# Expert weights in runs of 16 KB: four successive rows to a partition, and the turned rows of x and of the activations taken with a step of four columns

## The chip, the cores and the metric

The kernel runs on one core of one Trainium2 chip, in float32 throughout. The metric is the device time of one execution in microseconds (us), the median of three runs.

## The reference

One layer of a diffusion backbone with 128 context tokens and 512 latent tokens of 1024 features: adaLN modulation, two groups of attention heads, an output projection, and then an expert-choice mixture of 16 experts. The last part is the one that matters here:

```python
def expert_choice_moe(h, w_router, w_gate, w_up, w_down):
    B, T, D = h.shape
    cap = CAPACITY_FACTOR * T // N_EXPERTS
    logits = jnp.einsum('btd,de->bte', h, w_router, preferred_element_type=jnp.float32)
    aff = jax.nn.softmax(logits, axis=-1)
    g, idx = lax.top_k(jnp.swapaxes(aff, 1, 2), cap)
    xg = jax.vmap(lambda hb, ib: hb[ib])(h, idx)
    a = jnp.einsum('becd,edf->becf', xg, w_gate)
    u = jnp.einsum('becd,edf->becf', xg, w_up)
    y = jnp.einsum('becf,efd->becd', jax.nn.silu(a) * u, w_down) * g[..., None].astype(h.dtype)
    return jax.vmap(lambda yb, ib: jnp.zeros((T, D), yb.dtype).at[ib.reshape(-1)].add(yb.reshape(-1, D)))(y, idx)
```

`h = rms_norm(x, g_pre_ffn) * (1 + scale) + shift`, with shift and scale from the modulation. Each expert has three weights of 1024 x 1024 (4 MB each), takes 64 latent rows and 16 context rows, and is computed for both kinds of token.

## The kernel before

**Stages.** The weights of the modulation (`w_ada`), of the input projection and of the output projection come in units of 2 MB through a ring of six slots of 16 KB per partition. SyncE issues all these loads in the order of `UNITS`; between two of them, in `load_consts`, it issues ten small loads (sinks, router weights `wr`, gains). The projection loop runs over 15 products (`project`, L632 and L656), with the rest of the modulation (`ada`, L582) put between them. Attention follows, then the output projection (L810), the router, and the experts from about 394 us on.

**Experts.** An expert has six halves of 2 MB: gate, up and down, halves 0 and 1. `expert_weight` (L476) loads one: partition p takes rows 128c + p for four successive c, so a partition has four runs of 4 KB that lie 512 KB apart in memory. Up and down have two slots each in the ring, the gate weights four (two more slots in `reg2_qt`, named `reg_qt` in the profile). SyncE waits until TensorE has used a slot and then issues its next load (`refill`), in the order up(e+1), gate(e+3), down(e+1). Its waits are all that holds these loads back.

**TensorE's order.** `product_c` (L968) multiplies the context rows with one half, in 16 steps of 128 x 256 weights to four quarters of the output partitions; `product_l` (L954) does the latent rows in 16 steps of 128 x 512. The weights are the moving operand, 32 rows of x or of activations the stationary one. Each float32 product is two matmul instructions in the trace. `expert(e)` runs up(e), half 0 of gate(e+1), the transposes of the activations (L1008 for context, L1013 for latent rows), for even e the transposes of the next pair's rows (`turn_rows_l`, L933), half 1 of gate(e+1), and down(e). A transpose has its data as the stationary operand and the identity as the moving one.

**Gathers and scatters.** Rows of two experts at a time are fetched by an indirect DMA of 128 rows of 4 KB (`gather_l`, L1975), issued by GpSimd after the scatter of the expert before: `scatter(e)` (L2001 and L2003) adds 64 and 16 rows to sums in memory. `gather_c` (L1980) does the same for the context rows, once for each half of the experts. VectorE modulates the turned rows with `cmod` (`modulate`), a column for each feature block, which `columns` makes from `modq` turned by `mod_columns`.

Of the kernel before, what the change touches and what calls it, by code (L numbers as in the profile page):

```python
# [25 lines left out]
ALU = mybir.AluOpType  # L26
# [3 lines left out]
P = 128  # L30
D = 1024
KC = D // P
# [78 lines left out]
def build(nc, A, out):  # L111
    ctx = ExitStack()
    with ctx:
# [42 lines left out]
        rbias = sb("rbias", 2 * E)  # L156
        mhalf = sb("mhalf", 16)
        held = small[:, 110:111]

        def ring_slot(s):  # L160
            if s >= SLOTS:
                return reg2_qt[:, (s - SLOTS) * UNIT:(s - SLOTS + 1) * UNIT]
            return ring[:, s * UNIT:(s + 1) * UNIT]
# [210 lines left out]

        N_EARLY = 10
        N_KEYS = 7
        N_CONSTS = 10

        LOADS = [sum(UNITS[v][:2] != ("win", 0) for v in range(len(UNITS)) if slot_of(v) == s) for s in range(SLOTS)]
        block = ctx.enter_context(nc.Block())  # L380
# [3 lines left out]
        def _(sp):  # L384
# [19 lines left out]
            def load_consts():  # L404

                sp.dma_start(sink[:, :], A["sink_b"].to_broadcast([P, HEADS])).then_inc(consts_in, 16)
                sp.dma_start(wr[:, :].rearrange("p (c e) -> p c e", e=E),
                             A["w_router"][0].rearrange("(c p) e -> p c e", p=P)).then_inc(consts_in, 16)
                for n, name in enumerate(("g_post_attn", "g_post_ffn")):
                    rows = A[name].rearrange("a (q n) -> q a n", q=4)  # L410
                    for q in range(4):
                        sp.dma_start(gpost[32 * q:32 * q + 32, n * QUART:(n + 1) * QUART],
                                     rows[q].to_broadcast([32, QUART])).then_inc(consts_in, 16)
# [58 lines left out]

            def expert_weight(e, kind, half, s):
                w = (A["w_gate"], A["w_up"], A["w_down"])[kind]
                src = w[0].rearrange("e (c p) n -> e p c n", p=P)[e][:, 4 * half:4 * half + 4, :]
                sp.dma_start(ring_slot(s).rearrange("p (c n) -> p c n", c=4), src).then_inc(slot_in[s], 16)  # L476


            def store_x1(o):
# [59 lines left out]
        def _(pe):  # L539
# [47 lines left out]
            def mod_columns(n, m):  # L587

                pe.wait_ge(mod_ready, m + 3)
                pe.wait_ge(modcol_ready, n + 2)  # L590
                for j in range(2):
                    last = pe.transpose(ps[:, 7, j * P:(j + 1) * P], modq[:, m, j * P:(j + 1) * P], ident[:, :])
                last.then_inc(modcol_done, 1)

            pe.wait_ge(early_in, 16 * N_EARLY)
# [222 lines left out]
            def turn_x1(o, half):  # L818

                t = OUT_ORDER[o]  # L820
                pe.wait_ge(x1_ready, o + 1 + (half if o == TILES - 1 else 0))
                for c in range(4):
                    last = pe.transpose(out_at(o)[:, half, c * P:(c + 1) * P],
                                        xr[:, t, (4 * half + c) * P:(4 * half + c + 1) * P], ident[:, :])
                last.then_inc(x1_turned, 1)

            def route_logits(o):
# [94 lines left out]
            def turn_rows_c(g):  # L922

                pe.wait_ge(gathered_c, g * 16 + 16)
                for c in range(KC):
                    last = pe.transpose(ps[:, 5 + c // 4, c % 4 * P:(c % 4 + 1) * P], xg_c[:, c * P:(c + 1) * P], ident[:, :])
                last.then_inc(xc_turned, 1)

            def turn_rows_l(pair):

                pe.wait_ge(gathered_l, pair * 16 + 16)
                for c in range(KC):
                    last = pe.transpose(ps[:, 5 + c // 4, c % 4 * P:(c % 4 + 1) * P], xg_l[:, c * P:(c + 1) * P], ident[:, :])  # L933
                    if c % 4 == 3:
                        last.then_inc(xe_turned, 1)

# [19 lines left out]
                                             start=(hf == 0 and j == 0), stop=(hf == 1 and j == 3))  # L956
                return last

            def product_c(s, o, x, arriving=False):

                w = ring_slot(s).rearrange("p (c n) -> p c n", c=4)
                hf = s % 2
                for j in range(4):
                    c = 4 * hf + j
                    if arriving:
                        pe.wait_ge(xc_ready, c + 1)
                    for q in range(4):
                        last = pe.matmul(o[32 * q:32 * q + 32, :], x(c),  # L968
                                         w[:, j, q * QUART:(q + 1) * QUART], start=(c == 0), stop=(c == KC - 1))
                return last  # L970

            def rows_of(e):
# [20 lines left out]
            def expert(e):  # L993

                final = e == E - 1
                weight_in(2, e)
                pe.wait_ge(silu_done, e * 2 + 2)
                product_c(2, GC[:, QUART:], context_of(e))
                product_l(2, U, rows_of(e)).then_inc(up_a, 1)
                weight_in(3, e)  # L1000
                product_c(3, GC[:, QUART:], context_of(e)).then_inc(up_c, 1)
                product_l(3, U, rows_of(e)).then_inc(up_b, 1)
                pe.wait_ge(act_c_ready, e + 1)
                if not final:
                    gate_product(e + 1, 0)
                pe.wait_ge(y_ready, e + 1)
                for j in range(2):
                    last = pe.transpose(YC[:, QUART + j * P:QUART + (j + 1) * P], a_c[:, j * P:(j + 1) * P],  # L1008
                                        ident[:, :])
                last.then_inc(act_c_turned, 1)  # L1010
                pe.wait_ge(act_l_ready, e + 1)
                for j in range(4):
                    last = pe.transpose(TA[:, j * P:(j + 1) * P], a_l[:, j * P:(j + 1) * P], ident[:, :])  # L1013
                last.then_inc(act_l_turned, 1)
                if e % 2 == 0 and e + 2 < E:
                    pe.wait_ge(xe_ready, e + 2)
# [8 lines left out]
                product_c(4, YC[:, 0:QUART], acts_c)  # L1025
                if final:
                    weight_in(5, e)
                    product_c(5, YC[:, 0:QUART], acts_c).then_inc(down_c, 1)
# [7 lines left out]
                product_c(5, YC[:, 0:QUART], acts_c)  # L1036
# [26 lines left out]
            product_c(4, YC[:, 0:QUART], acts_c)  # L1063
            pe.wait_ge(xc_ready, KC + 1)
            turn_rows_l(0)
            weight_in(5, 0)
            product_c(5, YC[:, 0:QUART], acts_c)

            gate_l(0, 0)
            gate_l(0, 1)  # L1070
# [3 lines left out]
            gate_product(1, 0)  # L1074
            pe.wait_ge(act_l_ready, 1)
            for j in range(4):
                last = pe.transpose(TA[:, j * P:(j + 1) * P], a_l[:, j * P:(j + 1) * P], ident[:, :])
            last.then_inc(act_l_turned, 1)
            turn_rows_l(1)
            gate_product(1, 1)  # L1080
# [13 lines left out]
        def _(act):  # L1094

            act.dma_start(ident[:, :], A["identity"]).then_inc(early_in, 16)
            act.dma_start(gpre[:, :], A["g_pre_columns"]).then_inc(early_in, 16)
# [274 lines left out]
        def _(dve):  # L1372
            chain = [0]

            def link(ins):

                ins.then_inc(dve_step, 1)
                chain[0] += 1
                dve.wait_ge(dve_step, chain[0])
# [49 lines left out]
            cols = ps[:, 7, 0:2 * P].rearrange("p (j q r) -> p q j r", j=2, q=4)  # L1429

            def columns(m):
                n = COLS[m]
                dve.wait_ge(modcol_done, n + 3)
                for cond in (0, 1):
                    dst = cmod[:, n, cond, :].rearrange("p (q j) -> p q j", j=2)
                    if n % 2 == 0:
                        last = dve.tensor_copy(dst, cols[:, :, :, cond])
                    else:
                        g = gpre[:, (n // 2) * KC:(n // 2 + 1) * KC].rearrange("p (q j) -> p q j", j=2)
                        last = dve.scalar_tensor_tensor(dst, cols[:, :, :, cond], 1.0, g, ALU.add, ALU.mult)  # L1440
                last.then_inc(modcol_ready, 1)

            dve.wait_ge(early_in, 16 * N_EARLY)
# [653 lines left out]
```

## Time and profile before

| | |
|---|---|
| three runs | 948.62, 950.81, 950.79 us, median 950.79 us |
| profiled execution | 950.83 us, of it a span of 948.8 us |
| TensorE busy | 887.2 us, 94% of the span |
| weights of the experts | 96 loads of 2048 KB |
| moved over the span | 269.31 MB in 77717 packets |
| granted clock, mean | 0.986 of full speed |

The span runs from the first to the last instruction; 2.0 us of the execution lie around it. Busy TensorE means that a matmul is under way, not that it runs at its peak, so the pace of the products is read from the starts of the groups in the timeline. The DMA share is the mean busy share of 16 engines and can be a little over 1. A DMA's "landing" is the time from its issue until its semaphore is complete.

### The profile page before, as it was taken

The numbers are of one execution on the slowest core, as the hardware profiler recorded it, in microseconds if no ns is written. First come the engines' busy times: TensorE is split into PE (matmuls) and PEld (weight loads), VectorE is DVE, ScalarE is ACT, GpSimd is POOL, SyncE is SP. The second block draws the span as 40 slices with busy tenths as digits, with TensorE's granted clock in tenths as the row PEclk, the third lists the DMA queues.
The fourth block names the chain that finished last, engine by engine and source line by source line (L and its number), as shares of the span: only waits on it lengthen the run. The fifth ranks groups of instructions, "written<-read, shape, count | busy, mean of one in ns | idle before, by whom it ended". The sixth has DMA issues, their size and how long they took to land. (4 is left out here: it accounts for less than half of the span.)

```text
span 948.8 us, 19908 instructions
## 1 busy us (share of the span) xinstructions
PE 887.2 (94%) x8641; PEld 441.1 (46%) x8641; DVE 365.1 (38%) x974; ACT 216.3 (23%) x528; POOL 102.2 (11%) x137
## 2 busy tenths in 40 slices
PE   3999998899999999889999999999999999999984
PEld 3544444777656565633443443344344343433431
DVE  4255635887767765812031021111113120220135
ACT  3132223766544653410000000000000000000012
POOL 1021200000000000100011011011101101110225
PEclk9999999999899999999999999999999999999997
DMA  9997532300001115979999999999999999999984
GB/s 340 346 368 276 221 135 100 118 1 1 2 1 46 45 46 220 400 270 411 398 398 398 409 398 397 410 398 398 397 409 398 396 409 398 398 408 376 354 303 158
DMA packets 77717, 269.31 MB, mean 284 GB/s; under 512 B 6208, under 2 KB 9984, under 8 KB 77632
## 3 DMA queue, kind: packets, MB, share of 16 engines
q1 hardware_dynamic: 72384, 251.42, 67.7%
q0 software_dynamic: 4160, 13.90, 5.1%
q10 hardware_dynamic: 1088, 2.74, 0.7%
q8 instruction: 68, 1.11, 0.5%
q14 instruction: 17, 0.14, 0.0%
HBM read 252.06 MB, written 15.99 MB: 283 GB/s over the span
## 5 line engine op out<-in xcount | busy, mean ns | idle before, releaser
L954 PE MATMUL ps<-ring,reg 128*32 128x512 f32 x1792 | 201.6, 592 | 0.0
L1814 DVE TENSOR_SCALAR mod<-ps,kt 64x512 f32<-64x512 f32 x30 | 22.5, 749 | 260.6 <-PE ps L954 260.4
L954 PEld LDWEIGHTS ps<-ring,reg 128*32 128x32 f32 x1792 | 58.4, 110 | 113.0 <-issue 104.6
L968 PE MATMUL ps<-ring,values_in 128*32 128x256 f32 x1536 | 92.4, 382 | 4.6 <-DMA ring<-in_w_up 2.3
L1325 ACT ACTIVATE reg<-ps 128x256 f32<-128x256 f32 x16 | 6.2, 385 | 361.8 <-PE ps L1008 361.8
L954 PE MATMUL ps<-ring,kt 128*32 128x512 f32 x768 | 86.8, 592 | 0.0
L810 PE MATMUL ps<-ring,reg 128*128 128x512 f32 x160 | 78.1, 615 | 0.0
L968 PEld LDWEIGHTS ps<-ring,values_in 128*32 128x32 f32 x1536 | 49.3, 110 | 54.8 <-issue 14.6
L656 PE MATMUL ps<-ring,reg_qt 128*128 128x512 f32 x160 | 70.6, 594 | 0.0
L968 PE MATMUL ps<-ring,reg 128*32 128x256 f32 x1024 | 62.9, 388 | 5.6 <-DMA ring<-in_w_down 4.6
L1268 ACT ACTIVATE ring<-ps 128x640 f32<-128x640 f32 (+3 forms) x80 | 44.3, 554 | 74.9 <-PE ps L739 72.4
L739 PE MATMUL ps<-ident,ring 128*128 128x128 f32 x288 | 47.8, 285 | 13.9 <-DVE ring L1676 7.9
L1971 POOL TENSOR_TENSOR small<-mhalf 128x1 f32<-128x1 f32 x31 | 9.5, 306 | 460.8 <-DVE kt L1817 433.5
L1174 ACT ACTIVATE ring<-ps,small 128x640 f32<-128x640 f32 (+3 forms) x80 | 50.9, 637 | 8.1 <-DVE small L1576 8.0
L968 PEld LDWEIGHTS ps<-ring,reg 128*32 128x32 f32 x1024 | 32.5, 111 | 42.2 <-DMA ring<-in_w_down 18.8
L739 PEld LDWEIGHTS ps<-ident,ring 128*128 128x128 f32 x288 | 33.8, 144 | 37.8 <-issue 19.6
L954 PEld LDWEIGHTS ps<-ring,kt 128*32 128x32 f32 x768 | 25.4, 110 | 46.8 <-issue 42.8
L656 PEld LDWEIGHTS ps<-ring,reg_qt 128*128 128x128 f32 x160 | 29.6, 190 | 34.7 <-issue 34.7
L761 PE MATMUL ps<-ring,values_in 128*64 128x128 f32 x576 | 40.5, 281 | 0.6 <-ACT ring L1268 0.6
L810 PEld LDWEIGHTS ps<-ring,reg 128*128 128x128 f32 x160 | 29.1, 193 | 25.2 <-issue 24.5
L1676 DVE TENSOR_SCALAR ring<-ring,small 128x640 f32<-128x640 f32 (+3 forms) x80 | 36.8, 460 | 2.8
L632 PE MATMUL ps<-ring,reg_qt 128*128 128x512 f32 x80 | 35.9, 596 | 1.3 <-ACT reg_qt L1121 1.3
(238 smaller groups left out, 999.4 us busy)
## 6 DMA issues: line engine op xcount, KB each, us to landing
ring<-in_w_up SPq DMA_DIRECT2D x32, 2048.0 KB, 23.7
ring<-in_w_down SPq DMA_DIRECT2D x32, 2048.0 KB, 26.2
ring<-in_w_gate SPq DMA_DIRECT2D x16, 2048.0 KB
reg_qt<-in_w_gate SPq DMA_DIRECT2D x16, 2048.0 KB
ring<-in_w_ada SPq DMA_DIRECT2D x12, 2048.0 KB, 14.7
reg<-in_x_sample SPq DMA_DIRECT2D x8, 512.0 KB, 6.2
ring<-in_w_in SPq DMA_DIRECT2D x2, 2048.0 KB, 17.1
ring<-in_w_out SPq DMA_DIRECT2D x2, 2048.0 KB, 10.1
```

The source lines that it names most:

```text
L632: last = pe.matmul(projected(t), hT[:, c, t * P:(t + 1) * P], w[:, c, :], start=(c == 0), stop=(c == KC - 1))
L656: last = pe.matmul(projected(i), hT[:, c, t * P:(t + 1) * P], w[:, c, :], start=(c == 0), stop=(c == KC - 1))
L739: last = pe.transpose(two[2][:, b * P:(b + 1) * P], probs[:, u % 3, b * P:(b + 1) * P], ident[:, :])
L761: last = pe.matmul(ps[64 * hh:64 * hh + 64, bank, 0:P], v, pT[:, k % 2, hh, n * P:(n + 1) * P], start=(n == 0), stop=(n == len(blocks) - 1))
L810: last = pe.matmul(out_at(o)[:, n, :], attnT[:, c, t * P:(t + 1) * P], unit_at(wout_units[c // 4], 4)[:, c % 4, n * 512:(n + 1) * 512], st ...
L954: last = pe.matmul(o[64 * n + r:64 * n + r + 32, :], x(4 * hf + j, r), w[:, j, n * HALF:(n + 1) * HALF], start=(hf == 0 and j == 0), stop= ...
L968: last = pe.matmul(o[32 * q:32 * q + 32, :], x(c), w[:, j, q * QUART:(q + 1) * QUART], start=(c == 0), stop=(c == KC - 1))
L1174: act.activation(dst, scores_of(u), ACT.Exp, bias=negm[:, b:b + 1], scale=DH ** -0.5, accum_out=den[:, b:b + 1]).then_inc(exp_done, 1)
L1268: act.activation(pT[:, k % 2, u % 2, 0:n], two[2][:, 0:n], ACT.Copy).then_inc(pT_ready, 1)
L1676: dve.tensor_scalar(probs[:, u % 3, 0:n], probs[:, u % 3, 0:n], rden[:, b:b + 1], None, ALU.mult)\
L1814: dve.tensor_scalar(put_l[:, n * HALF:(n + 1) * HALF], ps[rows, 3, :], g_l[rows, e:e + 1], None, ALU.mult)
L1971: pool.tensor_tensor(held, mhalf[:, 0:1], mhalf[:, 1:2], ALU.add).then_inc(held_ops, 1)
```

## The change

A partition now takes four successive rows of a half: rows 512h + 4p + j for j = 0 to 3, one run of 16 KB in memory. The contraction of step j is then over the features 512h + 4p + j, and everything that meets these weights is laid out alike:

- rows of x (`turn_rows_c`, `turn_rows_l`), x1 for the router (`turn_x1`) and latent activations are turned with a step of four columns (16 bytes) in the stationary operand (`feature_block`);
- the context activations sit in quarters of the partitions, so `product_c` for gate and up reads the weights as moving operand with a step of four columns (`by_block`), two blocks of 128 for each quarter; for down it reads them as before;
- `mod_columns` makes four transposes of 64 columns where it made two of 128, `columns` four copies where it had two operations, and for the scale a wait on all constants, a link and two more operations;
- the router weights come in two loads with runs of 256 bytes instead of 64, and the gains of the second norm come in eight small loads of single elements through SyncE's queue, so `load_consts` issues 19 loads instead of ten.

```diff
+        def feature_block(row, c):
+
+            return row.rearrange("p (h q j) -> p h j q", h=2, j=4)[:, c // 4, c % 4, :]
...
-        N_CONSTS = 10
+        N_CONSTS = 19
...
-                sp.dma_start(wr[:, :].rearrange("p (c e) -> p c e", e=E),
-                             A["w_router"][0].rearrange("(c p) e -> p c e", p=P)).then_inc(consts_in, 16)
+                wr_rows = A["w_router"][0].rearrange("(h p j) e -> h p j e", h=2, j=4)
+                sp.dma_start(wr[:, 0:4 * E].rearrange("p (c e) -> p c e", e=E),
+                             wr_rows[0]).then_inc(consts_in, 16)
+                sp.dma_start(wr[:, 4 * E:].rearrange("p (c e) -> p c e", e=E), wr_rows[1]).then_inc(consts_in, 16)
+                ffn_columns = A["g_pre_columns"].rearrange("(q j) (m h b) -> b h m q j", j=4, m=2, h=2)
+                for b, h in itertools.product(range(4), range(2)):
+                    sp.dma_start(gpre[32 * b:32 * b + 32, KC + 4 * h:KC + 4 * h + 4], ffn_columns[b][h][1],
+                                 allow_slow_non_contiguous=True).then_inc(consts_in, 16)
...
-                src = w[0].rearrange("e (c p) n -> e p c n", p=P)[e][:, 4 * half:4 * half + 4, :]
-                sp.dma_start(ring_slot(s).rearrange("p (c n) -> p c n", c=4), src).then_inc(slot_in[s], 16)
+                src = w[0].rearrange("e (h p j) n -> e h p (j n)", h=2, j=4)[e][half]
+                sp.dma_start(ring_slot(s), src).then_inc(slot_in[s], 16)
...
-                for j in range(2):
-                    last = pe.transpose(ps[:, 7, j * P:(j + 1) * P], modq[:, m, j * P:(j + 1) * P], ident[:, :])
+                for j in range(4):
+                    last = pe.transpose(ps[0:P // 2, 7, j * P:(j + 1) * P], modq[:, m, j:QUART:4], ident[:, :])
...
-                    last = pe.transpose(ps[:, 5 + c // 4, c % 4 * P:(c % 4 + 1) * P], xg_l[:, c * P:(c + 1) * P], ident[:, :])
+                    last = pe.transpose(ps[:, 5 + c // 4, c % 4 * P:(c % 4 + 1) * P], feature_block(xg_l, c), ident[:, :])
...
+                by_block = ring_slot(s).rearrange("p (c h q j) -> p c h j q", c=4, h=2, j=4)
...
-                                         w[:, j, q * QUART:(q + 1) * QUART], start=(c == 0), stop=(c == KC - 1))
+                                         w[:, j, q * QUART:(q + 1) * QUART] if down else by_block[:, j, q // 2, 2 * (q % 2):2 * (q % 2) + 2, :],
+                                         start=(c == 0), stop=(c == KC - 1))
...
-                    last = pe.transpose(TA[:, j * P:(j + 1) * P], a_l[:, j * P:(j + 1) * P], ident[:, :])
+                    last = pe.transpose(TA[:, j * P:(j + 1) * P], a_l[:, j:HALF:4], ident[:, :])
...
-                    if n % 2 == 0:
-                        last = dve.tensor_copy(dst, cols[:, :, :, cond])
-                    else:
-                        g = gpre[:, (n // 2) * KC:(n // 2 + 1) * KC].rearrange("p (q j) -> p q j", j=2)
-                        last = dve.scalar_tensor_tensor(dst, cols[:, :, :, cond], 1.0, g, ALU.add, ALU.mult)
+                    for u in (0, 1):
+                        part = slice(P // 2 * u, P // 2 * (u + 1))
+                        last = dve.tensor_copy(cmod[part, n, cond, :].rearrange("p (h j) -> p h j", h=2), cols[:, u, :, :, cond])
+                if n % 2:
+                    dve.wait_ge(consts_in, 16 * N_CONSTS)
+                    link(last)
+                    for cond in (0, 1):
+                        g = gpre[:, (n // 2) * KC:(n // 2 + 1) * KC]
+                        last = dve.scalar_tensor_tensor(cmod[:, n, cond, :], cmod[:, n, cond, :], 1.0, g, ALU.add, ALU.mult)
```

## Rows read from the trace of the kernel before

**Rows 1.** Page: GB/s in 40 slices; the hardware DMA queue's packets and MB.

```profile
GB/s 340 346 368 276 221 135 100 118 1 1 2 1 46 45 46 220 400 270 411 398 398 398 409 398 397 410 398 398 397 409 398 396 409 398 398 408 376 354 303 158
...
q1 hardware_dynamic: 72384, 251.42, 67.7%
```

**Rows 2.** Windows: steady expert stretch; 2 KB pieces; 4 KB pieces; a late weight.

```profile
core 0: us, PE busy (x) PEld busy (x) DVE busy (x) ACT busy (x) POOL busy (x), PEclk, DMA share, GB/s
445.50:893.00 447.50, 439.59 (x5315) 179.81 (x5308) 83.19 (x150) 24.08 (x52) 50.98 (x58) 1.00 1.02 398
...
20.00:28.00 8.00, 4.53 (x77) 3.17 (x75) 3.86 (x11) 2.20 (x6) 0.00 (x0) 1.00 1.07 372
600.00:610.00 10.00, 9.45 (x120) 3.88 (x124) 0.00 (x0) 0.03 (x1) 0.00 (x0) 1.00 1.03 410
766.00:772.00 6.00, 4.09 (x40) 1.97 (x44) 0.00 (x0) 0.82 (x2) 0.00 (x0) 0.72 1.03 412
```

**Rows 3.** Timeline of TensorE in experts: start, length, line; idle before in brackets.

```profile
582.48 1.91 PE L968 MATMUL ps<-ring,values_in 128*32 128x256 f32 x32
584.21 3.62 PE L954 MATMUL ps<-ring,reg 128*32 128x512 f32 x32
587.64 1.91 PE L968 MATMUL ps<-ring,values_in 128*32 128x256 f32 x32
...
592.91 0.44 PE L1008 MATMUL ps<-ident,reg 128*128 128x128 f32 x2
...
593.72 1.93 PE L968 MATMUL ps<-ring,values_in 128*32 128x256 f32 x32
```

**Rows 4.** Timeline of TensorE where weights come late, and where gathered rows do.

```profile
506.92 3.62 PE L954 MATMUL ps<-ring,reg 128*32 128x512 f32 x32
511.79 1.93 PE L968 MATMUL ps<-ring,values_in 128*32 128x256 f32 x32 [1.25 <-DMA ring<-in_w_up]
...
627.93 1.06 PE L933 MATMUL ps<-ident,reg 128*128 128x128 f32 x8 [0.57 <-DMA reg<-rows_l,kt]
...
767.91 3.62 PE L968 MATMUL ps<-ring,reg 128*32 128x256 f32 x32 [2.02 <-DMA ring<-in_w_down]
771.30 3.67 PE L954 MATMUL ps<-ring,reg 128*32 128x512 f32 x32
```

**Rows 5.** Waits of TensorE from 390 us on: total, times, longest.

```profile
PE ps L968 <- DMA ring<-in_w_down: 4.6, 4, 2.0
...
PE ps L968 <- DMA ring<-in_w_up: 2.3, 2, 1.2
...
PE ps L933 <- DMA reg<-rows_l,kt: 2.0, 3, 1.0
```

**Rows 6.** Timeline of GpSimd around one gather.

```profile
615.50 1.42 POOL L2001 DMA_INDIRECT sum_l<-mod,kt  x1 [0.45 <-issue]
...
618.91 1.01 POOL L1975 DMA_INDIRECT reg<-rows_l,kt  x1 [0.15 <-issue]
```

**Rows 7.** Gathers L1975: all eight; landing of the first at 405.8 us; L1980's two.

```profile
L1975 POOL DMA_INDIRECT reg<-rows_l,kt x8: 950/1007/1011, 405.8 to 819.9; - x8
...
DMA to landing us min/median/max: 4.3/8.2/9.7
...
DMA to landing us min/median/max: 4.3/4.3/4.3
...
DMA to landing us min/median/max: 8.3/8.4/8.6
```

**Rows 8.** Timeline of SyncE's DMA issues early on, and the products behind them.

```profile
44.34 1.81 SPq L412 DMA_DIRECT2D gpost<-in_g_post_ffn  x4
46.20 2.91 SPq L447 DMA_DIRECT2D ring<-in_w_ada  x3
...
L582 PE MATMUL ps<-ring,reg x256: 379/379/403, 68.2 to 141.7; 128*32 128x256 f32 x128
```

**Rows 9.** Weight loads of a transpose (duration ns min/median/max).

```profile
L933 PEld LDWEIGHTS ps<-ident,reg x64: 138/141/143, 410.2 to 828.8; 128*128 128x128 f32 x64
```

More of the change, by code:

```diff
@@ L823, in turn_x1 @@
                     last = pe.transpose(out_at(o)[:, half, c * P:(c + 1) * P],
-                                        xr[:, t, (4 * half + c) * P:(4 * half + c + 1) * P], ident[:, :])
+                                        feature_block(xr[:, t, :], 4 * half + c), ident[:, :])
                 last.then_inc(x1_turned, 1)
@@ L925, in turn_rows_c @@
                 for c in range(KC):
-                    last = pe.transpose(ps[:, 5 + c // 4, c % 4 * P:(c % 4 + 1) * P], xg_c[:, c * P:(c + 1) * P], ident[:, :])
+                    last = pe.transpose(ps[:, 5 + c // 4, c % 4 * P:(c % 4 + 1) * P], feature_block(xg_c, c), ident[:, :])
                 last.then_inc(xc_turned, 1)
@@ L957, in product_l, with product_c @@
                 return last
-            def product_c(s, o, x, arriving=False):
+            def product_c(s, o, x, down=False, arriving=False):
                 w = ring_slot(s).rearrange("p (c n) -> p c n", c=4)
+                by_block = ring_slot(s).rearrange("p (c h q j) -> p c h j q", c=4, h=2, j=4)
                 hf = s % 2
@@ L1024, in expert @@
                 pe.wait_ge(actT_c_ready, e + 1)
-                product_c(4, YC[:, 0:QUART], acts_c)
+                product_c(4, YC[:, 0:QUART], acts_c, down=True)
                 if final:
                     weight_in(5, e)
-                    product_c(5, YC[:, 0:QUART], acts_c).then_inc(down_c, 1)
+                    product_c(5, YC[:, 0:QUART], acts_c, down=True).then_inc(down_c, 1)
                     pe.wait_ge(actT_l_ready, e + 1)
@@ L1035, in expert @@
                 weight_in(5, e)
-                product_c(5, YC[:, 0:QUART], acts_c)
+                product_c(5, YC[:, 0:QUART], acts_c, down=True)
                 product_l(5, Y, acts_l).then_inc(down_b, 1)
@@ L1062, in _ @@
             pe.wait_ge(actT_c_ready, 1)
-            product_c(4, YC[:, 0:QUART], acts_c)
+            product_c(4, YC[:, 0:QUART], acts_c, down=True)
             pe.wait_ge(xc_ready, KC + 1)
@@ L1066, in _ @@
             weight_in(5, 0)
-            product_c(5, YC[:, 0:QUART], acts_c)
+            product_c(5, YC[:, 0:QUART], acts_c, down=True)
             gate_l(0, 0)
@@ L1076, in _ @@
             for j in range(4):
-                last = pe.transpose(TA[:, j * P:(j + 1) * P], a_l[:, j * P:(j + 1) * P], ident[:, :])
+                last = pe.transpose(TA[:, j * P:(j + 1) * P], a_l[:, j:HALF:4], ident[:, :])
             last.then_inc(act_l_turned, 1)
@@ L1096, in _ @@
             act.dma_start(ident[:, :], A["identity"]).then_inc(early_in, 16)
-            act.dma_start(gpre[:, :], A["g_pre_columns"]).then_inc(early_in, 16)
+            act.dma_start(gpre[:, 0:KC], A["g_pre_columns"][:, 0:KC]).then_inc(early_in, 16)
             b_rows = A["b_ada"][0].rearrange("(m q n) -> q m n", m=N_MOD, q=4)
@@ L1427, in modulate_x @@
                                   ALU.mult, ALU.add).then_inc(ht_ready, 1)
-            cols = ps[:, 7, 0:2 * P].rearrange("p (j q r) -> p q j r", j=2, q=4)
+            cols = ps[0:P // 2, 7, :].rearrange("p (j h u r) -> p u h j r", j=4, h=2, u=2)
             def columns(m):
@@ L1434, in columns @@
                 for cond in (0, 1):
-                    dst = cmod[:, n, cond, :].rearrange("p (q j) -> p q j", j=2)
-                    if n % 2 == 0:
-                        last = dve.tensor_copy(dst, cols[:, :, :, cond])
-                    else:
-                        g = gpre[:, (n // 2) * KC:(n // 2 + 1) * KC].rearrange("p (q j) -> p q j", j=2)
-                        last = dve.scalar_tensor_tensor(dst, cols[:, :, :, cond], 1.0, g, ALU.add, ALU.mult)
+                    for u in (0, 1):
[7 more added lines that the diff above has]
+                        last = dve.scalar_tensor_tensor(cmod[:, n, cond, :], cmod[:, n, cond, :], 1.0, g, ALU.add, ALU.mult)
                 last.then_inc(modcol_ready, 1)
```

## Prediction, made before the changed kernel was run

> **What bounds the kernel now.** I looked first at the slices of the page, then at windows, then at TensorE's timeline. From about 0.43 of the span on the DMA engines move some 400 GB/s in nearly every slice [rows 1]: the weights of the experts. From 445.5 to 893 us the DMA share is 1.02, and TensorE is busy for 439.59 of 447.5 us [rows 2]. Both look full, so the timeline decides. One half of a weight costs TensorE 1.73 us for L968 and 3.43 us for L954, from start to start, 5.16 us in all [rows 3]. Six halves are 30.96 us, the transposes between the two products add some 0.9 us, and turning a pair's rows (1.0 us) comes every second expert, so an expert needs about 32.3 us. Its 12.6 MB at the 410 GB/s of a window with weights alone [rows 2] take 30.7 us, and scatters and gathers come on top. The two are level; TensorE sets the end, and now and then a half is late.
>
> What the lateness costs: TensorE waited for weights 4.6 + 2.3 us in six places [rows 5]. From 506.92 to 511.79 us is 4.87 us where 3.43 are usual, so a wait listed with 1.25 costs 1.44; six such excesses make 6.9 + 1.2 = 8.1 us. After the longest wait (2.02 us) L968 took from 767.91 to 771.30, 3.39 us instead of 1.75 [rows 3, 4], with a granted clock of 0.72 over that window [rows 2], so partly at 1.2 GHz: 1.64 us more. Together 9.7 us. That is nearly all that faster weight loads can give back.
>
> The third thing to see is the gather L1975. It is issued at 618.91, 3.4 us after the scatter of its expert [rows 6], and TensorE, which goes through a fixed sequence meanwhile, reaches L933 about 8.4 us after the issue: it began at 627.93 after a wait of 0.57 [rows 4]. The gather lands after 8.2 us in the median [rows 7]. It has no slack. With SyncE's queue idle, as at 405.8 us, the same gather landed after 4.3 us; beside weight loads it takes up to 3.9 us (median) longer.
>
> **The weight loads.** The hardware queue moves 251.42 MB in 72384 packets, 3.5 KB on average [rows 1]: one packet for each run of 4 KB. 16 engines at 410 GB/s make 0.160 us for a 4 KB packet; in the window with mostly 2 KB pieces the rate is 372, so 0.088 us for 2 KB [rows 2]. The line through both has 0.016 us per packet; a packet of 16 KB would take 0.59 us by it, 0.64 at the rate of 4 KB. I take 0.61, some 4 to 5% more bandwidth. An expert's loads then take about 29.3 us against 32.3 for TensorE, and the 9.7 us of late weights go: -9.7 (bounds -9.7 and 0).
>
> **The gathers behind larger packets.** A gather has 128 rows of 4 KB on 16 engines, eight packets each; the scatters ahead of it have 4 and 1. If an engine takes turns between its queues packet by packet, each of these 13 waits for one weight packet: now 0.16 us, after the change 0.61. That makes the landing 13 x 0.45 = 5.9 us later. From both sides: only the gather's own eight waits count, 3.6 us; or all of the 3.9 us between the idle and the loaded queue [rows 7] grows with the packet, by a factor 3.8, which adds 10.9 us. No row here has packets over 4 KB, so zero is possible too (a rival). I take 5.9, next to the lower count. The median landing becomes 14.1 us, and TensorE stands for 14.1 - 8.4 = 5.7 us at L933, with the whole rest of the expert behind it. This happens for experts 2, 4, ... 12, six times: 34.2 us, less the 1.0 us that these gathers cost now (2.0 in L933's row less 1.0 at the first, where the queue was idle [rows 5]): +33.2. The weight queue is not idle then: up and gate of later experts are issued just before the gather. After a stop of 5.7 us the clock should fall as it did after 2.02: 6 x 1.64 = +9.8 (low 0: most waits of 1 to 1.5 us cost none). `gather_c` lands after 8.3 to 8.6 us [rows 7] beside the first expert's weights; its first one is waited for, eight packets: +3.6, the second falls behind most of the loads: 0.
>
> The Trainium skill (DMA: Bandwidth & Descriptors, "Queues, rings and completion order") says that an engine goes round robin between queue rows and changes only at a packet's end. By that the delay above comes; without it the sum would be without the 46.6 us. The difference between 4.3 and 8.2 us agrees with some such taking of turns, but does not show its unit.
>
> **Strided reads.** `product_c` for gate and up reads its moving operand with a step of 16 bytes: 64 halves of 1.73 us. Upper bound: each takes twice as long, +111 us. Lower bound 0. The nearest row: 32 instructions in groups of four in 1.73 us are 0.216 us for 256 columns [rows 3], 0.84 ns or two cycles of 2.4 GHz for a column. At one float32 every second cycle I take 0. In the transposes the strided operand is the stationary one: 144 of them in the experts (64 and 16 for gathered rows, 64 for activations) and 40 for x1 beside the output projection. Their loads take 0.141 us [rows 9]; twice that would be up to +26 us, and I take 0 here too.
>
> The Trainium skill (SBUF — State Buffer, "Door 1: The DMA port swizzle") has lines of 16 bytes and a penalty where each access goes to a new one. Here each does, so by that page the sum is up to 137 us higher; no row of before reads this way.
>
> **The rest.** `mod_columns` makes four transposes more in all, some 0.5 us on TensorE. `columns` has ten small operations more on VectorE at perhaps 0.16 us, which run behind TensorE's projections; without that cover 2 us. The wait on the constants is met long before. SyncE issues nine loads more before `w_ada`: four took 1.81 us [rows 8], so it moves from 46.2 to about 51. The previous 2 MB load is still in flight then, and its weights are first used at 68.2 [rows 8]. Nothing, and 5 us if the cover is gone. Router weights in larger runs save packets, tiny loads add some: nothing.
>
> **The sum.** -9.7 + 33.2 + 9.8 + 3.6 + 0.5 = +37.4. The profiled execution took 950.83 us (its span 948.8), the median is 950.79, so the forecast is 988.2 us.
>
> **Rivals.** (a) The gathers are late, as above: 0.47. With the low counts (3.6 us each, three clock falls) 6 x 3.4 - 1.0 + 4.9 + 3.6 - 9.7 + 0.5 gives 969; with 7 us or more each it goes past 995. Own range 962 to 1005. (b) Weights are no longer late and nothing takes their place: 950.8 - 9.7 + 0.5 = 941.6, faster: 0.29. For it speaks the full DMA share; against it that the gather has no slack. It decides as soon as a gather's landing grows by less than some 1.5 us. (c) A run of 16 KB is cut into the same 4 KB packets, so the loads don't change: 950 to 952, 0.12; the pieces then lie together in memory, so half of this may still be a little faster. (d) Strided reads cost TensorE time: from 64 halves at 1.5 times upward, 1000 to 1080 us, 0.12. It needs no DMA at all; the memory port behind 32-row tiles, which four products use at once, is not seen at its limit in any row.
>
> **How the numbers follow.** 988.2 is (a)'s. The range must hold (b), (c) and most of (a): 938 to 1006. A measurement of this kernel tells 0.3%, 3 us. Faster: (b) and a part of (c), 0.34; same: 0.08; slower: (a) and (d), 0.58.
>
> **What the profile after would show.** Packets of the hardware queue fall from 72384 to about 35500 (96 loads with 384 fewer each); if not, (c). The windows give 420 GB/s or more while loads run, and TensorE's waits for weights go. The landing of L1975 beside loads rises from 8.2 to about 14 us, and TensorE waits some 5.7 us at L933 six times, with the clock low behind it; landings under 9.5 us make (a) wrong. L968 stays at 1.73 us and L933's weight loads at 0.141 us; if not, (d). The forecast fails if the packets are large but the queues share an engine in finer steps than a packet.

## The result, and the profile after

The changed kernel takes 1064.51 us in the median of four runs (1064.17 to 1064.9), beside 950.8 us for the kernel before on the same chip: a ratio of 1.1213, interval 1.1188 to 1.1237, that is 113.7 us slower. The forecast was 988.2 us with a range of 938 to 1006. The sign was right and the size was not: the time lies in rival (d)'s band.

The page of the profile after, the two rows that answer to [rows 1]:

```profile
GB/s 346 279 398 299 184 2 192 2 1 1 21 41 40 133 422 81 414 415 415 325 347 331 318 339 326 330 340 325 332 335 317 343 325 317 349 325 169 267 247 149
...
q1 hardware_dynamic: 35920, 251.42, 61.3%
```

The same 251.42 MB go in 35920 packets (forecast: about 35500), so a run of 16 KB is one packet and rival (c) is out. But where before had about 400 GB/s in nearly every slice of the experts, most slices from the twentieth on now have 317 to 349. The windows, as in [rows 2]:

```profile
445.50:893.00 447.50, 447.50 (x4377) 168.25 (x4379) 69.62 (x126) 21.69 (x47) 38.57 (x43) 1.00 0.91 340
450.00:460.00 10.00, 10.00 (x98) 3.24 (x92) 0.00 (x0) 0.87 (x2) 0.00 (x0) 1.00 1.01 431
460.00:466.00 6.00, 6.00 (x60) 2.20 (x56) 3.41 (x6) 0.00 (x0) 1.40 (x2) 1.00 1.02 434
```

While loads are in flight they move at 431 and 434 GB/s, above the 410 of 4 KB pieces; over the whole stretch the DMA share is only 0.91. So the loads wait for buffers, not the products for loads. SyncE's waits for TensorE in `expert_weight` say the same, first before, then after, from 390 us on:

```profile
SPq L476 <- PE ps L954: 96.2, 27, 12.3
```

```profile
SPq L486 <- PE ps L964: 553.6, 88, 19.9
```

TensorE is busy for all 447.5 us, at full clock, and does 4377 instructions in that time where it did 5315 before. It has become slower at the same work. Its timeline says where, as in [rows 3] and [rows 4]:

```profile
587.05 3.82 PE L979 MATMUL ps<-ring,values_in 128*32 128x256 f32 x32
...
594.11 3.81 PE L979 MATMUL ps<-reg_qt,values_in 128*32 128x256 f32 x32
...
602.05 1.13 PE L943 MATMUL ps<-ident,reg 128*128 128x128 f32 x8
...
610.17 1.91 PE L979 MATMUL ps<-ring,reg 128*32 128x256 f32 x32
611.89 3.62 PE L964 MATMUL ps<-ring,reg 128*32 128x512 f32 x32
...
620.49 3.80 PE L979 MATMUL ps<-ring,values_in 128*32 128x256 f32 x32
624.08 3.64 PE L964 MATMUL ps<-ring,reg 128*32 128x512 f32 x32
627.53 3.83 PE L979 MATMUL ps<-ring,values_in 128*32 128x256 f32 x32
631.16 3.64 PE L964 MATMUL ps<-ring,reg 128*32 128x512 f32 x32
```

L979 is `product_c` (L968 before), L964 `product_l` (L954). The L979 of 610.17 is a down product, which reads plainly: 1.72 us from its start to the next. The two of 620.49 and 627.53 read gate or up with the step of 16 bytes: 3.59 and 3.63 us, 3.61 in the mean and 1.88 more than 1.73. L964 keeps 3.44 us. There are 64 stepped halves, and 64 x 1.88 is 120.3 us. That is the result, with a few us of smaller terms beside it (the section on why the prediction was wrong).

The waits of TensorE from 390 us on, as in [rows 5]:

```profile
PE ps L936 <- DMA mod<-rows_c,kt: 4.6, 1, 4.6
...
PE ps L943 <- DMA reg<-rows_l,kt: 0.3, 1, 0.3
```

No wait for a weight is left, as forecast. But the gathered rows (L943, L933 before) aren't late either. The timeline of GpSimd has the issue of the gather for the L943 of 602.05, as in [rows 6]:

```profile
587.98 1.01 POOL L1990 DMA_INDIRECT reg<-rows_l,kt  x1 [0.15 <-issue]
```

The groups of its line and of L943's weight loads, as in [rows 7] and [rows 9]:

```profile
L1990 POOL DMA_INDIRECT reg<-rows_l,kt x8: 951/1008/1017, 415.7 to 908.8; - x8
...
DMA to landing us min/median/max: 4.4/11.4/12.7
...
L943 PEld LDWEIGHTS ps<-ident,reg x64: 196/212/227, 420.2 to 923.6; 128*128 128x128 f32 x64
```

The landing did grow, from 8.2 to 11.4 us, though not to the 14 of the forecast. But TensorE now needs 14.07 us from the issue to L943 (587.98 to 602.05), where it needed 8.4: the slow halves hide the late gather. Of the two costs that I had added up, the larger covers the other.

### The profile page after: what moved, and what is told of

Its sections match the earlier page's. It is cut to its first block, busy times and chain, and to the rows that moved or that the text cites. A ratio compares the mean times of both kernels' runs of the same rounds, so it can differ in the third digit from the quotient of the medians.

```text
span 1062.2 us, 19932 instructions
## 1 busy us (share of the span) xinstructions
PE 1007.5 (95%) x8645; PEld 468.7 (44%) x8645; DVE 366.2 (34%) x980; ACT 216.0 (20%) x528; POOL 102.0 (10%) x137
## 3 DMA queue, kind: packets, MB, share of 16 engines
q1 hardware_dynamic: 35920, 251.42, 61.3%
## 4 chain that ended last, share of the span: by engine, by line
PE 58%; POOL 1%; DMA 0%; issue 0%; DVE 0%; ACT 0%; POOLq 0%; ACTq 0%; DVEq 0%
PE ps L964 30%; PE ps L979 26%; PE ps L943 1%; PE ps L1025 1%; PE ps L1020 0%; POOL small L2047 0%; DMA reg<-rows_l,kt 0%; POOL small L1938 0%; ACT ring L1366 0%; POOL out L2054 0%; POOL out L2058 0%; DVE ring L1879 0%; DVE reg L1813 0%; PE ps L1089 0%; DVE reg_qt L1886 0%
## 5 line engine op out<-in xcount | busy, mean ns | idle before, releaser
L964 PE MATMUL ps<-ring,reg 128*32 128x512 f32 x1792 | 202.4, 593 | 0.0
L979 PE MATMUL ps<-ring,values_in 128*32 128x256 f32 x1536 | 183.7, 633 | 2.2 <-ACT reg L1333 1.1
L964 PEld LDWEIGHTS ps<-ring,reg 128*32 128x32 f32 x1792 | 62.3, 112 | 118.3 <-issue 113.3
L979 PEld LDWEIGHTS ps<-ring,values_in 128*32 128x32 f32 x1536 | 58.5, 125 | 112.2 <-issue 109.1
L964 PE MATMUL ps<-ring,kt 128*32 128x512 f32 x768 | 87.6, 594 | 0.0
L666 PE MATMUL ps<-ring,reg_qt 128*128 128x512 f32 x160 | 70.6, 595 | 0.0
L979 PE MATMUL ps<-ring,reg 128*32 128x256 f32 x1024 | 61.9, 383 | 1.0 <-ACT reg L1337 1.0
L979 PE MATMUL ps<-reg_qt,values_in 128*32 128x256 f32 x512 | 61.5, 633 | 0.0
L749 PE MATMUL ps<-ident,ring 128*128 128x128 f32 x288 | 47.6, 284 | 14.1 <-DVE ring L1691 7.8
L964 PEld LDWEIGHTS ps<-ring,kt 128*32 128x32 f32 x768 | 28.5, 114 | 55.3 <-issue 55.3
L979 PEld LDWEIGHTS ps<-ring,reg 128*32 128x32 f32 x1024 | 34.1, 111 | 34.2 <-issue 17.9
L1808 DVE TENSOR_TENSOR reg<-reg,ps 128x256 f32<-128x256 f32 x15 | 6.3, 422 | 97.4 <-PE ps L979 97.4
```

The costliest lines, as they stand in the source:

```text
L666: last = pe.matmul(projected(i), hT[:, c, t * P:(t + 1) * P], w[:, c, :], start=(c == 0), stop=(c == KC - 1))
L749: last = pe.transpose(two[2][:, b * P:(b + 1) * P], probs[:, u % 3, b * P:(b + 1) * P], ident[:, :])
L964: last = pe.matmul(o[64 * n + r:64 * n + r + 32, :], x(4 * hf + j, r), w[:, j, n * HALF:(n + 1) * HALF], start=(hf == 0 and j == 0), stop= ...
L979: last = pe.matmul(o[32 * q:32 * q + 32, :], x(c), w[:, j, q * QUART:(q + 1) * QUART] if down else by_block[:, j, q // 2, 2 * (q % 2):2 * ...
```

## The experiments

**Only the steps, or only the runs.** The first run keeps the changed kernel and takes the step out of the moving operand. Its context rows then meet the features in another order, so it doesn't compute the reference; it is there for its time:

```
 for q in range(4):
     last = pe.matmul(o[32 * q:32 * q + 32, :], x(c),
-                     w[:, j, q * QUART:(q + 1) * QUART] if down else by_block[:, j, q // 2, 2 * (q % 2):2 * (q % 2) + 2, :],
+                     w[:, j, q * QUART:(q + 1) * QUART],
```

> The changed kernel with one thing undone: product_c reads the gate and up weights with no step, so the context rows of the experts come out with their features in another order. Runs of 16 KB and all stepped transposes stay. Theory A (the step of the moving operand costs 1.9 us in each of 64 halves, 120 us): L979 goes back to 1.73 us from start to start for all weights; the late weights stay away (-9.7); the gathers of latent rows land after 11.4 us or more, as after the change, but now TensorE arrives after 8.4 us, so it waits some 3 to 4 us at L943 six times; with some falls of the clock 960 to 975 us. Theory B (the 16 KB runs themselves, as they land, slow TensorE's reads or hold it up elsewhere; the step is free): 1050 to 1065 us, L979 at 3.6 us for gate and up.

The second keeps the kernel before, its loads of 4 KB pieces too, and puts in the step alone (the same line the other way round). It too leaves the context features in another order.

> The kernel before with one thing added: product_c reads the gate and up weights with the step of four columns; loads in runs of 4 KB, plain transposes. It leaves the context rows' features in another order. Theory A: 950.8 + 64 x 1.88 - up to 9.7 (weights are no longer late, since an expert takes 7.5 us longer than its loads) = 1061 to 1065 us. Theory B: 950 to 953 us.

Measured: 994.41 us for plain reads on 16 KB runs (ratio 1.0459, 1.0415 to 1.0503) and 1058.7 us for steps on 4 KB pieces (1.1149, 1.1109 to 1.1189), beside 948.45 for before. The timeline of the second; L970 is its `product_c`, L954 its `product_l`:

```profile
614.29 3.84 PE L970 MATMUL ps<-ring,values_in 128*32 128x256 f32 x32
617.94 3.62 PE L954 MATMUL ps<-ring,reg 128*32 128x512 f32 x32
```

3.65 us for a stepped half with nothing of the loads changed: the step alone does it. 120.3 us less the 9.7 of late weights, which a slower TensorE no longer meets, is 110.6; measured are 110.3. (The forecast of 1061 to 1065 us started from 950.8; beside 948.45 it would be 2.3 lower.) The whole change costs 113.7, so 3.4 us are left for the larger packets, near the 3.9 more that the wait for `gather_c` costs.

The first run came out 19 us above Theory A's 960 to 975: I had taken over the landing of 11.4 us from the changed kernel, and it is 14.1 here. It is my forecast's case (a), undisturbed. Its timeline of TensorE behind a gather that was issued at 565.36, its waits, its windows there, and the landing of L1990:

```profile
573.20 0.65 PE L1025 MATMUL ps<-ident,reg 128*128 128x128 f32 x4
580.01 1.95 PE L943 MATMUL ps<-ident,reg 128*128 128x128 f32 x8 [6.17 <-DMA reg<-rows_l,kt]
581.90 2.65 PE L979 MATMUL ps<-reg_qt,values_in 128*32 128x256 f32 x32
584.37 3.61 PE L964 MATMUL ps<-reg_qt,reg 128*32 128x512 f32 x32
```

```profile
PE ps L943 <- DMA reg<-rows_l,kt: 36.3, 7, 6.2
PE ps L936 <- DMA mod<-rows_c,kt: 4.3, 1, 4.3
```

```profile
575.00:580.00 5.00, 0.00 (x0) 0.02 (x1) 0.00 (x0) 0.00 (x0) 0.00 (x0) 0.66 1.02 433
580.00:584.00 4.00, 3.99 (x36) 2.65 (x40) 2.67 (x4) 0.00 (x0) 0.00 (x0) 0.57 0.89 381
```

```profile
DMA to landing us min/median/max: 4.3/14.1/14.6
```

TensorE stands still for 6.17 us (6.2 at most) while the DMA engines move 433 GB/s, mostly weights that nobody waits for. Its granted clock is 0.66 in the window of the stop and 0.57 in the next, so most of that time is at 1.2 instead of 2.4 GHz, and the next two groups take 1.89 and 2.47 us from start to start instead of the 1.06 and 1.75 behind the L943 of 439.20, which had no wait: 1.6 us more. This is the cheapest of the six long stops. Read in the same way, with the L964 behind, those at 506.26, 652.78, 726.53, 799.13 and 872.60 cost 2.6, 2.7, 1.7, 2.9 and 2.0 us, so the low clock costs 13.4 us in all. The median landing is 14.1 us, the value of the forecast.

The trace also shows how the gather comes to be late. The two DMA queues from 572 to 577 us, while the gather is moving (packets, MB, share of 16 engines):

```profile
q1 hardware_dynamic: 120, 1.72, 81.1%
q0 software_dynamic: 122, 0.47, 22.8%
```

1.72 MB are 105 weight packets of 16 KB, 0.47 MB some 114 gather packets of 4 KB; the rest are tiny. So about one weight packet goes for each packet of the gather, which is the turn-taking that the forecast had assumed.

**What a step costs.** The kernel before with a block of unused products ahead of the experts, which read one ring slot at steps of 1, 2, 3, 4 and 8 elements, as whole tiles and as four strips of 32 columns; then transposes with the stepped read as the stationary operand. For each step:

```
+for _ in range(4):
+    pe.matmul(ps[:, 3, :], full, stream[:, 0:512 * step:step], start=True, stop=True)
...
+for n in range(32):
+    pe.matmul(ps[32 * (n % 4):32 * (n % 4) + 32, 3, 0:256], strips[n % 4],
+              stream[:, 1024 * (n % 4):1024 * (n % 4) + 256 * step:step], start=True, stop=True)
...
+for _ in range(16):
+    pe.transpose(ps[:, 3, 0:P], stream[:, 0:P * step:step], full)
```

> The kernel before with a block of extra products ahead of the experts, whose results nobody uses, one line for each kind: full tiles 128 x 512 with moving step 1, 2, 3, 4, 8; strips of 32 columns, four at once, 128 x 256 with step 1, 2, 3, 4; 16 transposes with stationary step 1, 2, 3, 4, 8. If each access to a new line of 16 bytes costs (theory A1), full tiles are at 0.43 us per instruction at step 1 and 0.86 or more at step 4 and 8, with steps 2 and 3 cheap or between. If it is four strips reading at once that overload the memory (A2), full tiles stay at 0.43 us at any step and only the strips double. In the transposes, weight loads of about 0.14 us at step 1 and 0.21 at step 4.

It was executed once. Its timeline of TensorE: L1060 to L1068 are the whole tiles at steps 1, 2, 3, 4, 8; L1070 to L1076 the strips at 1, 2, 3, 4; L1078 to L1086 the transposes at 1, 2, 3, 4, 8:

```profile
402.57 3.60 PE L1060 MATMUL ps<-ring,ident 128*128 128x512 f32 x8
406.00 3.76 PE L1062 MATMUL ps<-ring,ident 128*128 128x512 f32 x8
409.61 5.57 PE L1064 MATMUL ps<-ring,ident 128*128 128x512 f32 x8
415.01 7.37 PE L1066 MATMUL ps<-ring,ident 128*128 128x512 f32 x8
422.20 7.53 PE L1068 MATMUL ps<-ring,ident 128*128 128x512 f32 x8
429.65 3.66 PE L1070 MATMUL ps<-ring,ident 128*32 128x256 f32 x64
433.13 3.87 PE L1072 MATMUL ps<-ring,ident 128*32 128x256 f32 x64
436.76 5.71 PE L1074 MATMUL ps<-ring,ident 128*32 128x256 f32 x64
442.25 7.47 PE L1076 MATMUL ps<-ring,ident 128*32 128x256 f32 x64
449.65 1.97 PE L1078 MATMUL ps<-ident,ring 128*128 128x128 f32 x16
...
455.21 2.10 PE L1084 MATMUL ps<-ident,ring 128*128 128x128 f32 x16
457.15 1.95 PE L1086 MATMUL ps<-ident,ring 128*128 128x128 f32 x16
```

From start to start the whole tiles take 3.43, 3.61, 5.40, 7.19 and 7.45 us for 8 x 512 columns: 0.84, 0.88, 1.32, 1.76 and 1.82 ns per column. Count the 16-byte lines that a column touches on average: a quarter, a half, three quarters, one, one. From step 2 on that is 1.76 to 1.82 ns per line; at step 1 the 0.84 ns of the column itself are the longer limit. The strips take 3.48, 3.63, 5.49 and 7.40 us for 16 groups of four, the same per column. So it is the reading of one operand, and that four strips run side by side changes nothing: the theory that the four reads of a group share a port fell. The stepped half of the changed kernel, 8 groups x 256 columns in 3.61 us, is 1.76 ns per column too. Transposes with a stepped stationary operand take 1.80 us for 16 at step 1 and 1.94 at step 4. Their weight loads take 141 ns in the median at step 1 and 212 at step 4, and nearly as much at steps 2, 3 and 8 (209, 200, 193).

The Trainium skill (SBUF — State Buffer, "Door 1: The DMA port swizzle") has lines of 16 bytes and a penalty for each access that crosses into a new one. The run agrees on the line, 0.84 ns against 1.76. The same place lets float32 stride by up to four for free; here a step of 3 costs 1.32 and a step of 4 costs 1.76, and the measurement decides.

**Are the late gathers worth 49 us, and are large packets their cause?** Three runs. The first issues the gathers one expert earlier, ahead of an expert's scatters, on the plain-read kernel of the first run:

```
-if e % 2 == 0 and e + 2 < E:
-    pool.wait_ge(xe_turned, e + 2)
-    gather_l(e // 2 + 1)
+for pair in [1, 2] if e == 0 else [e // 2 + 2] if e % 2 == 0 and e + 4 < E else []:
+    pool.wait_ge(xe_turned, 2 * pair)
+    gather_l(pair)
```

> e1 (runs of 16 KB for all weights, no step in product_c, context features in another order) with the earlier gather of e6 and e8. It prices the late gathers by themselves: if they are the whole of e1's 994.4 us beyond the gains, the waits at L943 (36.3 us) and the falls of the clock behind them (mean clock 0.965, against 0.986 to 0.99) go, and the time is 942 to 950 us; the first gather of context rows still costs some 4 us. If TensorE is held by something else in large packets, 955 or more.

That kernel, like the first run, leaves the context features in another order. The other two need a version with plain reads that computes the whole, and it is measured too. Context activations are turned with a step of four into two partition halves, and ScalarE's copy goes in four pieces; all weights come in 16 KB runs:

```
-    last = pe.transpose(YC[:, QUART + j * P:QUART + (j + 1) * P], a_c[:, j * P:(j + 1) * P], ident[:, :])
+    if j < 2:
+        pe.transpose(YC[0:P // 2, k:k + P], a_c[:, j:QUART:4], ident[:, :])
+    else:
+        last = pe.matmul(YC[P // 2:P, k:k + P], a_c[:, j:QUART:4], ident[:, :], start=True, stop=True)
```

> The changed kernel, whole computation, with plain reads of gate and up: the context activations keep their natural order and are turned with a step of four columns into two halves of the partitions (two transposes, two plain products with the identity), and ScalarE copies them in four pieces. Theory A: within 3 us of the first run of this call, 960 to 978 us, against 1064.5 for the change; ahead of the kernel before only if TensorE's waits at L943 stay under 1.5 us each. Theory B: no gain over 1064.5.

Then the same kernel with each half loaded as two DMAs whose runs are 4 KB, to the same places:

```
-sp.dma_start(ring_slot(s), src).then_inc(slot_in[s], 16)
+for b in (0, 1):
+    sp.dma_start(ring_slot(s).rearrange("p (a b n) -> p b a n", a=2, b=2)[:, b], src[b]).then_inc(slot_in[s], 16)
```

> The fix (e4, whole computation) with the same rows in the same places, but each half loaded by two DMAs whose patterns cannot be joined into runs over 4 KB. Only the size of a packet differs from e4. Theory P (each packet of a gather waits behind one weight packet, so the packet's size makes the gather late): the gathers of latent rows land after 8 to 9 us again instead of 14, the waits at L943 fall from 32.6 us to under 3, and with fewer falls of the clock the time is 962 to 975 us. Theory Q (the order of rows in memory, or the stepped transposes, make it late): landing stays near 14 us and the time near 1005.

And again with 16 KB runs, but the early gather:

> The fix (e4) with each gather of latent rows issued one expert earlier, ahead of the scatter before it: its buffer is free by then. Theory P: the landing may stay at 10 to 14 us, but TensorE no longer stands at L943; 1004.9 - 32.6 - some 8 for the clock = 962 to 968 us. If something other than the gather's lateness holds TensorE there, 990 or more.

Measured, with the landing of the gather of latent rows and TensorE's waits for them:

| kernel | us | ratio to before (interval) | landing, median | waits for latent rows |
|---|---|---|---|---|
| plain reads, 16 KB | 994.41 | 1.0459 (1.0415 to 1.0503) | 14.1 | 36.3 us, 7 times |
| the same, early gather | 945.14 | 0.9964 (0.9951 to 0.9976) | 12.3 | 1.2 us, once |
| whole computation, 16 KB | 1004.87 | 1.058 (1.0531 to 1.0628) | 14.6 | 32.6 us, 6 times |
| the same, 4 KB pieces | 954.19 | 1.0052 (1.0035 to 1.0068) | 8.0 | none |
| the same, 16 KB, early gather | 958.15 | 1.0091 (1.0073 to 1.0108) | 12.2 | none |

With the same reads, products and places in memory, loads in runs of 4 KB, two DMAs for a half instead of one, move the landing from 14.6 to 8.0 us and the time from 1004.87 to 954.19. The packets of the hardware queue go from 35920 to 74320 with it. And with large packets left as they are, giving the gather more time takes 49.3 us off (994.41 to 945.14) and 46.7 off (1004.87 to 958.15). The runs of a pair were made on different chips; taken each against the kernel before beside it, the early gather gives 50.0 and 47.8 us and the 4 KB runs 51.8. Cause and price agree from both sides. The profiled executions of the first pair lie 50.6 us apart (996.44 and 945.87). Of these the traces place 36.3 less 1.2 in waits and 13.4 in the low clock; the last 2.1 are not placed. The whole computation costs 10.5 to 13.0 us over the plain-read kernels: from the start of the turning of an expert's activations to the next product it takes 1.72 us instead of 0.85. That makes 13.9 us for 16 experts, and the forecast for the whole computation, within 3 us of the first run, had left it out. The forecasts for the two others were too high: 962 to 975 us for the 4 KB runs, 962 to 968 for the early gather. The second had allowed 8 us for the clock, where 46.7 less the 32.6 us of waits leave 14.1; and with 4 KB runs the wait for the first `gather_c`, 4.6 us in the whole computation on 16 KB runs, is 0.2.

The changed kernel less the early plain-read kernel is 1064.51 - 945.14 = 119.4 us, against 64 x 1.88 = 120.3; each against its own kernel before, it is 117.8. Either way the step is all of the loss within 3 us, and in the changed kernel the gathers of latent rows cost nothing beyond 0.3 us.

**Does the early gather help by itself?** The kernel before with only that edit.

> The kernel before, whole computation, with the earlier gather alone. Its gathers cost TensorE 1.0 us in all beside loads, so 947 to 951 us, no difference that can be told; the late weights (6.9 us of waits) stay, since the loads still go in 4 KB packets.

949.25 us beside 949.19 (1.0, 0.9989 to 1.0011), with weight waits of 6.9 and 1.7 us in it. Its gathers weren't late, so nothing was to be had.

**A version with both.** Gate and up in 16 KB runs, down in 4 KB pieces as before. Then the activations need no stepped turning, and the gate and up products no stepped read; only rows of x are turned with a step:

```
 def expert_weight(e, kind, half, s):
     w = (A["w_gate"], A["w_up"], A["w_down"])[kind]
+    if kind == 2:
+        src = w[0].rearrange("e (c p) n -> e p c n", p=P)[e][:, 4 * half:4 * half + 4, :]
+        sp.dma_start(ring_slot(s).rearrange("p (c n) -> p c n", c=4), src).then_inc(slot_in[s], 16)
+        return
...
-    last = pe.transpose(TA[:, j * P:(j + 1) * P], a_l[:, j:HALF:4], ident[:, :])
+    last = pe.transpose(TA[:, j * P:(j + 1) * P], a_l[:, j * P:(j + 1) * P], ident[:, :])
```

> Whole computation: runs of 16 KB for gate and up alone, the down weights as before in runs of 4 KB. So activations are turned as in the kernel before, and no moving operand has a step; rows of x are turned with a step of four. By P the gathers meet gate and up weights in 16 KB packets and land after 12 to 15 us: 980 to 996 us. Against the plain-read version of the first call (994.4) at most some us less.

And with the early gather:

> e7 with the earlier gather. No waits at L943. 950.8 - 9.7 (late weights) + 4 (first gather of context rows late) + 1 to 3 (slower weight loads of the stepped transposes) = 944 to 951 us: level with the kernel before or just ahead. If the late weights come back, since down is loaded in small packets, up to 955.

Measured: 940.73 us beside 949.52 (0.9897, 0.9876 to 0.9919), 0.8 to 1.2% faster than the kernel before and so the fastest here, and 942.04 (0.9919, 0.9903 to 0.9936) with the early gather, no better. The first one's waits of TensorE, its steady window, the landing, and SyncE's issues around the gather of 552.78:

```profile
PE ps L1106 <- ACT reg_qt L1375: 3.7, 2, 2.5
PE ps L947 <- DMA reg<-rows_l,kt: 2.2, 4, 1.0
```

```profile
445.00:880.00 435.00, 433.71 (x5270) 180.19 (x5266) 82.49 (x149) 24.08 (x52) 50.30 (x58) 1.00 1.01 408
```

```profile
DMA to landing us min/median/max: 4.3/8.3/13.0
```

```profile
539.85 5.54 SPq L487 DMA_DIRECT2D ring<-in_w_down  x2
550.30 6.26 SPq L490 DMA_DIRECT2D ring<-in_w_up  x2
```

TensorE is busy for 433.71 of 435 us, and no weight is waited for: the 9.7 us of the forecast's first term are what is gained (8.8). I had expected 980 to 996 us, with landings of 12 to 15 us and waits, and was wrong; the first two gathers landed after 4.3 and 13.0 us, the other six after 7.8 to 8.9. The large packets of up are issued just before, but the down loads of 539.85 lie ahead of them in the queue. The DMA queues from 557 to 561 us, beside the gather, show that it is those that move:

```profile
DMA packets 426, 1.63 MB, mean 407 GB/s; under 512 B 35, under 2 KB 35, under 8 KB 424
...
q1 hardware_dynamic: 265, 1.06, 64.8%
```

All but two of the 426 packets are under 8 KB. With the early gather the landing is 11.4 us again and costs nothing. That version came out 2 us below its forecast of 944 to 951: the 4 us for the first `gather_c` did not arise, as no wait for it is over 0.4 us.

## Why the prediction was wrong, step by step

- **The step that failed: "At one float32 every second cycle I take 0".** The bound above it, each of the 64 halves twice as long, was the truth: 1.73 became 3.61 us, +120.3 (the bound said +111). The row of before gave the time of a plain column, 0.84 ns, and I took it for what a read can do at any step. It is what four columns of one line can do; a line costs 1.76. The rival had a chance of 0.12, on the ground that no row showed the port at its limit. But none of the rows taken from before reads a float32 moving operand with a step, so none could show it; the two bounds were equally open and a value at one of them was not earned. The rule of the Trainium skill (SBUF — State Buffer, "Door 1: The DMA port swizzle") that stood beside it was the only sign that spoke for the upper end, and I had told half of it: the other half lets float32 stride by up to four for free. By the half told the sum was up to 137 us higher, 111 of them in `product_c`, where the step has cost 120.3.
- **Late weights, -9.7: right.** No wait for a weight is left. In the changed kernel that shows little, since steps on 4 KB pieces leave none either: TensorE is slower than the loads. But the plain-read kernels on 16 KB runs have none, and the mixed version gains 8.8 us. The packet of 16 KB takes 16 x 16384 B / 434 GB/s = 0.604 us; taken were 0.61.
- **Gathers behind larger packets, +33.2, and the clock, +9.8: right in mechanism and near in size, absent in this kernel.** The plain-read kernel has the landing at 14.1 us as forecast, 36.3 us of waits where 34.2 were forecast, and 13.4 us of low clock at six stops where 9.8 were taken; giving the gather time is worth 49.3 us, where the sum had 43.0. In the changed kernel three stepped halves lie between the end of the down product that starts the scatter (579.97) and L943 (602.05): 22.1 us instead of the 16.3 of the plain-read kernel (557.34 to 573.68). GpSimd goes at its own pace meanwhile, so its gather gains 5.7 us, the size of the stop. The landing is shorter besides, 11.4 us against 14.1. From 586 to 590 us, as the gather is issued, the weight queue moves 0.59 MB where 410 GB/s would be 1.64, and the scatters ahead land after 6.7 us in the median instead of 9.8; so the pause between loads is the likely reason, though no run tried it alone. The terms were treated as if they added; the larger hides the smaller.
- **`gather_c`, +3.6: right.** One wait of 4.6 us at L936, 3.9 more than before.
- **Transposes with a stepped weight load, 0: nearly right as a sum, wrong as a row.** The load of L943 went from 141 to 212 ns, not 141 as forecast, but 16 transposes need 1.94 us instead of 1.80. For the 184 stepped ones that would be 1.6 us.
- **Order of issues, 0: right.** `w_ada` moves from 46.2 to 50.74 us (forecast about 51), and nothing waits for it.
- **The sum with the right value** for the step: -9.7 + 3.6 + 0.5 + 120.3 = +114.7, with the gathers hidden. Measured are +113.7. The 0.5 for `mod_columns` was not measured by itself.

## What to carry to other kernels

Before the layout of a load is changed for larger packets, follow it to every operand that will then be read with a step: a float32 moving operand at a step of four takes twice as long as a plain one, and 1.9 us in each of 64 products outweighed the 9.7 us that faster loads could give back. Larger packets sped the queue that has them and delayed the other queue on the same engines, so look for the transfer with no slack beside it, and give it time or keep the packets small next to it. When two costs fall in the same stretch, ask first whether one hides the other, before they are added.

## What was unexpected in the hardware

- A moving operand of float32 costs TensorE about 1.76 ns for each 16-byte line that it touches, or 0.84 ns per column where that is more. Whole tiles and four strips side by side pay the same: 1.76 and 1.81 ns at a step of four.
- The same step on the stationary operand costs 71 ns more for a weight load (141 to 212) and little of the pace of transposes (1.80 to 1.94 us for 16). A step of two costs nearly the same (209).
- One run of 16 KB is one packet, and such packets reach 431 to 434 GB/s where 4 KB ones reached 410. The gather beside them lands after 14.1 us, beside 4 KB ones after 8.2, with the queue idle after 4.3. About one weight packet goes for each packet of the gather.
- SyncE is no longer held up by the issue of a weight half. The groups of `expert_weight`'s line, duration in ns (min/median/max), first in the kernel before, then after:

```profile
L476 SPq DMA_DIRECT2D ring<-in_w_up x32: 318/4698/9702, 366.7 to 888.1; - x32
```

```profile
L486 SPq DMA_DIRECT2D ring<-in_w_up x32: 328/333/530, 365.1 to 995.3; - x32
```

0.33 us in the median, where it was 4.7. No row of waits names SyncE's issue, so it brought nothing that these runs show. Either change frees it alone. With steps on 4 KB pieces the packets are small, but the weight queue is short (a load lands after 9.9 us in the median, 25.3 before). With plain reads, 16 KB runs and the early gather the queue is nearly as long as before (22.2 us), but the packets are large. The same groups of these two:

```profile
L476 SPq DMA_DIRECT2D ring<-in_w_up x32: 367/373/3688, 364.8 to 988.8; - x32
```

```profile
L486 SPq DMA_DIRECT2D ring<-in_w_up x32: 328/333/517, 365.3 to 883.1; - x32
```

So the long issue needs both, many small packets and a long queue.
